# Ten RMS norms split between ScalarE and VectorE, eight layer norms reordered, and the last store cut in halves

## The reference, cut to what matters

```python
def layer_norm(x, g, b, eps=1e-5):
    mu = jnp.mean(xf, -1, keepdims=True)
    var = jnp.mean(jnp.square(xf - mu), -1, keepdims=True)
    return ((xf - mu) * lax.rsqrt(var + eps) * g + b).astype(x.dtype)

def rmsnorm(x, g):
    y = x32 * lax.rsqrt(jnp.mean(x32 * x32, axis=-1, keepdims=True) + RMS_EPS)
    return (y * g.astype(jnp.float32)).astype(x.dtype)
...
    x = layer_norm(ALPHA * x + mix, ln1_g[l], ln1_b[l])      # layers 0, 1
    x = layer_norm(ALPHA * x + ffn, ln2_g[l], ln2_b[l])
...
    h = rmsnorm(x, attn_norm[layer])                         # layers 2, 3
    x = x + mixed @ w_o[layer]
    h = rmsnorm(x, ffn_norm[layer])
    x = x + conv_ffn(h, w_up[layer], conv_w[layer], conv_b[layer], w_down[layer])
return rmsnorm(x, final_norm)
```

## Time and profile before

| | us |
|---|---|
| median of the runs | 1466.06 |
| the profiled execution, its own time | 1465.25 |
| its span in the trace | 1463.5 |
| TensorE busy | 1389.7 (95%) |
| VectorE busy | 976.4 (67%) |
| ScalarE busy | 700.4 (48%) |
| mean granted TensorE clock | 0.978 |

### The profile page before, as it was taken

The page is one execution under the profiler, slowest core; times in us unless marked ns, Lnnn a source line. Parts: engine busy times, 40 slices in busy tenths (PEclk is TensorE's granted clock), DMA queues, the critical chain, the costliest instruction groups (busy, mean ns, idle before and its releaser), DMA issues.

```text
span 1463.5 us, 24482 instructions
## 1 busy us (share of the span) xinstructions
PE 1389.7 (95%) x10006; PEld 1285.3 (88%) x10006; DVE 976.4 (67%) x1660; ACT 700.4 (48%) x1149; POOL 85.1 (6%) x79
## 2 busy tenths in 40 slices
PE   9998899999999898999998999999999999999997
PEld 7997689999899777999987998889998899889996
DVE  5766775555759466655565685787768555786777
ACT  4755444334385543434344544455545454454453
POOL 0320000000014000000000011120000000000000
PEclk9999999999999899999998999999999999999999
DMA  8742245555443213655533434345454433445441
GB/s 317 276 150 87 87 147 195 177 192 183 166 155 137 91 59 121 225 175 195 178 131 142 145 116 145 134 163 183 180 200 159 173 123 132 157 157 206 187 173 58
DMA packets 38343, 233.22 MB, mean 159 GB/s; under 512 B 4984, under 2 KB 8776, under 8 KB 11864
## 3 DMA queue, kind: packets, MB, share of 16 engines
q1 hardware_dynamic: 36168, 224.18, 43.2%
q0 software_dynamic: 2064, 7.47, 1.6%
HBM read 230.55 MB, written 1.09 MB: 158 GB/s over the span
## 4 chain that ended last, share of the span: by engine, by line
PE 82%; DVE 10%; ACT 4%; issue 2%; POOL 0%; DMA 0%; SPq 0%; DVEq 0%; ACTq 0%
PE bank L746 24%; PE bank L747 24%; PE bank L748 23%; DVE w_lo L582 2%; PE bank L850 2%; ACT w_hi L572 1%; PE bank L930 1%; PE bank L952 1%; PE bank L954 1%; PE bank L953 1%; DVE a_lo L603 1%; DVE nstat L1555 1%; PE bank L826 1%; DVE arena L1630 0%; ACT a_hi L598 0%
## 5 line engine op out<-in xcount | busy, mean ns | idle before, releaser
L582 DVE TENSOR_TENSOR w_lo<-raw,w_hi 128x1024 fp32r<-128x1024 f32 x404 | 484.9, 1237 | 97.4 <-ACT w_hi L572 94.2
L746 PE MATMUL bank<-a_hi,w_hi 128*128 128x256 f32 x1856 | 530.0, 286 | 3.1 <-DVE w_lo L582 3.1
L747 PE MATMUL bank<-a_lo,w_hi 128*128 128x256 f32 x1856 | 525.9, 283 | 0.0
L748 PE MATMUL bank<-a_hi,w_lo 128*128 128x256 f32 x1856 | 525.8, 283 | 0.0
L572 ACT ACTIVATE w_hi<-raw 128x1024 fp32r<-128x1024 f32 x404 | 406.3, 1050 | 97.6 <-PE bank L748 89.6
L746 PEld LDWEIGHTS bank<-a_hi,w_hi 128*128 128x128 f32 x1856 | 356.4, 192 | 7.4 <-issue 4.4
L747 PEld LDWEIGHTS bank<-a_lo,w_hi 128*128 128x128 f32 x1856 | 356.5, 192 | 1.3
L748 PEld LDWEIGHTS bank<-a_hi,w_lo 128*128 128x128 f32 x1856 | 356.6, 192 | 0.0
L746 PE MATMUL bank<-w_hi,a_hi 128*128 128x256 f32 (+1 forms) x512 | 168.8, 330 | 16.3 <-DVE a_lo L603 15.5
L747 PE MATMUL bank<-w_lo,a_hi 128*128 128x256 f32 (+1 forms) x512 | 161.8, 316 | 0.0
L748 PE MATMUL bank<-w_hi,a_lo 128*128 128x256 f32 (+1 forms) x512 | 161.3, 315 | 0.0
(11 more groups left out here) (248 smaller groups left out, 1484.4 us busy)
## 6 DMA issues: line engine op xcount, KB each, us to landing
raw<-in_stream SPq DMA_DIRECT2D x201, 1024.0 KB, 4.9
bias_t<-bias_rows SPq DMA_DIRECT2D x6, 512.0 KB, 7.0
heads_buf<-in_w SPq DMA_DIRECT2D x2, 1024.0 KB, 7.9
gains<-in_w SPq DMA_DIRECT2D x2, 1024.0 KB, 10.0
gains<-in_ln_g POOLq DMA_DIRECT2D x4, 512.0 KB, 3.9
gains<-in_ln_b POOLq DMA_DIRECT2D x4, 512.0 KB, 5.7
gains<-in_rms_g POOLq DMA_DIRECT2D x3, 512.0 KB, 3.8
res<-in_xT SPq DMA_DIRECT2D x4, 256.0 KB, 5.2
```

Source lines behind the costliest of these rows:

```text
L582: dve.tensor_tensor(w_lo[:, i % PARTS, half_tile(h)], raw[:, i % SLOTS, half_tile(h)], w_hi[:, i % PARTS, half_tile(h)].bitcast(F32), ALU. ...
L746: pe.matmul(out, lh, rh, start=first, stop=False)
L747: pe.matmul(out, lh, rl, start=False, stop=False)
L748: return pe.matmul(out, ll, rh, start=False, stop=last)
```

## The change

RMS norms (4 to 8): ScalarE squares each half and sums the squares along the row in the same instruction, takes the root, and scales the first half; VectorE makes the first half's share of the mean square plus epsilon (a 128x1 operation), multiplies the first half by the gain while ScalarE squares, inverts the root, and scales the second half. TensorE waits for the first half on a semaphore of its own. Layer norms (0 to 3): the pass that subtracts the mean and multiplies by the gain now stands ahead of the wait for the root. The last store is issued in four pieces of 256 KB, each as its half is done. POOL's wait ahead of a load of gains asks for the same event in the new count.

```diff
@@ scalar: root
+                if n < 4:
+                    act.wait_ge(sum_done, sum_done_at(n, tt))
+                    act.activation(st[:, 14:15], st[:, 13:14], ACT.Sqrt, bias=eps_ln[:, 0:1]).then_inc(root_done, 1)
+                    return
+                for hf in range(2):
+                    if n == 4:
+                        act.wait_ge(normed, normed_by(3, tt, hf))
+                    else:
+                        act.wait_ge(acc_drained, sum_of(n) * PIECES + piece(tt, hf))
+                    act.activation(res[:, tt, half_rows(hf)], x[:, tt, half_rows(hf)], ACT.Square,
+                                   accum_out=st[:, hf:hf + 1]).then_inc(squares_done, 1)
+                act.wait_ge(squares_done, 2 * rms_no(n, tt) + 2)
+                act.wait_ge(half_sum, rms_no(n, tt) + 1)
+                act.activation(st[:, 14:15], st[:, 1:2], ACT.Sqrt, scale=1.0 / D,
+                               bias=st[:, 2:3]).then_inc(root_done, 1)
+                act.wait_ge(half_scaled, rms_no(n, tt) + 1)
+                act.wait_ge(rstd_done, rms_no(n, tt) + 1)
+                act.activation(res[:, tt, half_rows(0)], res[:, tt, half_rows(0)], ACT.Copy,
+                               scale=st[:, 15:16]).then_inc(first_normed, 1)
@@ vector
+            def rms_norm(n, tt):
+                st, no = nstat[:, tt, :], rms_no(n, tt)
+                if n > 4:
+                    for hf in range(2):
+                        residual(n, tt, hf)
+                    dve.wait_ge(gains_in, 16 * (8 + n - 4))
+                else:
+                    dve.wait_ge(gain4_in, 16)
+                first, second = [gain4[:, half_rows(hf)] if n == 4 else gains[:, 0, half_rows(hf)] for hf in range(2)]
+                dve.wait_ge(squares_done, 2 * no + 1)
+                dve.tensor_scalar(st[:, 2:3], st[:, 0:1], 1.0 / D, 1e-6, ALU.mult, ALU.add).then_inc(half_sum, 1)
+                dve.tensor_tensor(res[:, tt, half_rows(0)], x[:, tt, half_rows(0)], first,
+                                  ALU.mult).then_inc(half_scaled, 1)
+                dve.wait_ge(root_done, root_at(n, tt))
+                dve.reciprocal(st[:, 15:16], st[:, 14:15]).then_inc(rstd_done, 1)
+                dve.wait_ge(rstd_done, no + 1)
+                dve.scalar_tensor_tensor(res[:, tt, half_rows(1)], x[:, tt, half_rows(1)], st[:, 15:16], second,
+                                         ALU.mult, ALU.mult).then_inc(normed, 1)
...
-                dve.wait_ge(root_done, sum_done_at(n, tt))
-                step(dve.reciprocal(st[:, 15:16], st[:, 14:15]))
...
+                    step(dve.scalar_tensor_tensor(res[:, tt, c], res[:, tt, c], st[:, 12:13], gains[:, 0, c],
+                                                  ALU.subtract, ALU.mult))
+                    if hf == 0:
+                        dve.wait_ge(root_done, root_at(n, tt))
+                        step(dve.reciprocal(st[:, 15:16], st[:, 14:15]))
+                    dve.scalar_tensor_tensor(x[:, tt, c], res[:, tt, c], st[:, 15:16], gains[:, 1, c], ALU.mult,
+                                             ALU.add).then_inc(normed, 1)
@@ sync
             for tt in range(NT):
-                sp.wait_ge(normed, 8 * PIECES + piece(tt, 1))
-                sp.dma_start(a["out"][:, tt, :], res[:, tt, :]).then_inc(out_sem, 16)
-            sp.wait_ge(out_sem, 16 * NT)
+                for hf in range(2):
+                    wait_normed(sp, 8, tt, hf)
+                    sp.dma_start(a["out"][:, tt, half_rows(hf)], res[:, tt, half_rows(hf)]).then_inc(out_sem, 16)
+            sp.wait_ge(out_sem, 16 * PIECES)
```

More of the change, by code:

```diff
@@ L483, in build @@
         normed = sem("normed")
+        first_normed = sem("first_normed")
+        squares_done = sem("squares_done")
+        half_sum = sem("half_sum")
+        half_scaled = sem("half_scaled")
+        rstd_done = sem("rstd_done")
         gains_in = sem("gains_in")
@@ L549, in normed_by, with rms_no, wait_normed, root_at @@
         def normed_by(n, tt, hf):
+            if n < 3:
+                return n * PIECES + piece(tt, hf)
             if n in (3, 4):
-                return 3 * PIECES + 4 * tt + 2 * (n - 3) + hf + 1
-            return n * PIECES + piece(tt, hf)
+                return 3 * PIECES + 3 * tt + (n - 3) + hf + 1
+            return 3 * PIECES + 3 * NT + NT * (n - 5) + tt + 1
+        def rms_no(n, tt):
+            return NT * (n - 4) + tt
+        def wait_normed(eng, n, tt, hf):
+            if n >= 4 and hf == 0:
+                eng.wait_ge(first_normed, rms_no(n, tt) + 1)
+            else:
+                eng.wait_ge(normed, normed_by(n, tt, hf))
         def sum_done_at(n, tt):
+            return n * NT + tt + 1
+        def root_at(n, tt):
             return 3 * NT + 2 * tt + n - 2 if n in (3, 4) else n * NT + tt + 1
@@ L1531, in choose, with residual @@
                     step(dve.match_replace(part, stat[:, 8:16], part, TAKEN))
+            def residual(n, tt, hf):
+                c = half_rows(hf)
+                at = sum_of(n) * PIECES + piece(tt, hf)
+                dve.wait_ge(acc_full, at)
+                acc = bank[:, 4 + 2 * tt + hf, :]
+                if n == 0:
+                    dve.wait_ge(x_rows_in, 2 * 16)
+                if 0 < n < 4:
+                    dve.wait_ge(normed, normed_by(n - 1, tt, hf))
+                if n < 4:
+                    dve.scalar_tensor_tensor(res[:, tt, c], x[:, tt, c], ALPHA, acc, ALU.mult,
+                                             ALU.add).then_inc(acc_drained, 1)
+                else:
+                    dve.tensor_tensor(x[:, tt, c], x[:, tt, c], acc, ALU.add).then_inc(acc_drained, 1)
+                return at
@@ L1533, in norm @@
             def norm(n, tt):
+                if n >= 4:
+                    rms_norm(n, tt)
+                    return
                 st = nstat[:, tt, :]
                 for hf in range(2):
[L1537 to L1554 removed]
@@ L1555, in norm @@
-                    ins = dve.bn_stats(st[:, 6 * hf:6 * hf + 6], rows)
-                step(ins)
-                if n < 4:
-                    dve.bn_aggr(st[:, 12:14], st[:, 0:12]).then_inc(sum_done, 1)
-                else:
-                    step(dve.bn_aggr(st[:, 12:14], st[:, 0:12]))
-                    dve.scalar_tensor_tensor(st[:, 13:14], st[:, 12:13], st[:, 12:13], st[:, 13:14], ALU.mult,
-                                             ALU.add).then_inc(sum_done, 1)
-                dve.wait_ge(root_done, sum_done_at(n, tt))
@@ L1565, in norm @@
-                step(dve.reciprocal(st[:, 15:16], st[:, 14:15]))
-                if n == 4:
-                    dve.wait_ge(gain4_in, 16)
-                else:
-                    dve.wait_ge(gains_in, 2 * 16 * (n + 1) if n < 4 else 16 * (8 + n - 4))
+                    dve.wait_ge(acc_drained, residual(n, tt, hf))
+                    ins = dve.bn_stats(st[:, 6 * hf:6 * hf + 6], res[:, tt, half_rows(hf)])
+                step(ins)
+                dve.bn_aggr(st[:, 12:14], st[:, 0:12]).then_inc(sum_done, 1)
@@ L1903, in next_gains @@
             def next_gains(n, g, b=None):
[L1904 removed]
+                pool.wait_ge(normed, normed_by(n - 1, NT - 1, 1))
                 load_gains(g, b)
```

35 lines of the change are left out of this document (3 added, 32 removed).

## The result

In the same comparison the kernel before took 1467.53 us (median of five runs, 1465.76 to 1473.11) and the changed one 1456.39 (five runs, 1455.92 to 1460.28). The ratio is 0.9922, with an interval of 0.9903 to 0.9942: 11 us less, where 6.6 were forecast. The changed kernel was measured twice more among the experiments, with ratios of 0.9933 and 0.9948, so its gain is better read as 0.5 to 0.8% than as this one number. The median of its 18 runs in the three comparisons is 1459.2 us.

A forecast was written before the change was run, and what follows sets the result against it. TensorE bounds the kernel (82% of the 1463.5 us span), so only its waits count. Savings of 3.4 + 0.3 + 0.7 + 1.2 + 1.0 = 6.6 us from 1465.25 give 1458.65, with the median's 0.81 1459.5; range 1456.5 to 1463.5.

The forecast's parts named there:

- norms 5 to 7: Token group 1's transposes behind these RMS norms start earlier, saving 3.4 us in three places, between 2.4 and 4.0.
- The saving of 1.14 a place: Norms 5, 6 and 7, group 1: transposes could start at 939.83 instead of 940.97, leaving 0.19 us of stall.
- a sign of being wrong that the prediction had named: The prediction is wrong if VectorE's multiplication by the gain holds up the inversion; running 0.1 longer delays it 0.1.
- Rival 3: ScalarE's 512-column instructions with sum or column scale run far slower than the copy: 1473 us; chance 0.04 with anything else slower.
- The clock: Behind norm 6, with the stall all but gone, the clock stays up: 1.0 us saved, between 0 and 1.4.
- Rival 1: The clock gives back more: one more fall avoided, such as norm 1 group 1, 2 us more, 1457.5; chance 0.2.
- The base: The profiled execution's 1465.25 us, with 0.81 added because the median stands that far above it.
- Norms 3 and 4: Group 0's transposes 1.5 us late behind ScalarE's splits, group 1's path shorter: 0.3 us saved, between -0.9 and 1.2.
- The end: Behind the last norm, earlier store issue (0.8) and a smaller last transfer (0.6): 1.2 us taken, between 0.8 and 1.4.
- the landing: Last store: landing takes 2.6 us again, and 256 KB less in the last transfer saves another 0.6 us.
- Layer norms: Root's wait hidden behind a pass, 0.32 us at each of three places; 0.7 us taken, between 0.5 and 1.0.
- Rival 4: VectorE multiplies faster, so halving the scaling gains nothing; norms 5 to 7 give 2.5, 1460.4 us; within the forecast's 0.55 chance.

The follow-up runs named there:

- filled: Extra identity products on TensorE ahead of norms' transposes: ratio 0.9933 (1461.7 us) added to the kernel before, 0.9911 (1457.05 us) added to the changed kernel.
- the kernel before again: The kernel before, executed once more with nothing changed: median 1470.11 us over 10 runs, ratio 1.0008, profiled span 1468.1 us.

## Why the prediction was right or wrong

**Where the difference lies.** The result of 1456.39 us is the profiled execution itself, 8.9 us less than the profiled execution before, where 6.6 were forecast: 2.3 of the 3.1 us between forecast and result. The other 0.8 is what the forecast added for the median. Of the 2.3, norm 1's clock gives +2.3, norm 6's +0.2, the other stretches +0.8, and the rest of the sum -1.0 together (end -0.5, norms 3 and 4 -0.3, layer norms -0.1, norms 5 to 7 -0.1).

**Direction and path: right.** Squares of 512 columns take 0.61 to 0.63 us with 0.19 for the read, 0.73 from start to start of what follows; the scaling by a column takes 0.72; the root 0.29. All were taken so. The saving of 1.14 a place came at norms 6 and 7 (1.15, 1.14); at norm 5 it was 0.99, since there the root stands at 936.06, 2.15 us behind the addition instead of 2.08, and the inversion at 936.48. VectorE's small operation starts only at 935.81 there, so the multiplication by the gain ends at 936.56, behind the root's end at 936.35, and the inversion comes 0.1 us late: a sign of being wrong that the prediction had named, though a small one. What holds the small operation up at norm 5 alone isn't shown. Three places: 3.3 us against 3.4. Rival 3, slow forms, is dead by the same rows.

**The clock: the step that failed.** It said of norm 6 that "with that stall all but gone I expect the clock to stay up, as it did behind norms 5 and 7 with the stall", and counted 1.0 us for it "between 0 and 1.4". The first half came true (1.2 us). What was wrong is "as it did behind norms 5 and 7": it took one execution's clock for the kernel's. In how many profiled executions the clock fell behind each norm, leaving out those that were filled there (norm 1 goes by the layer norms' order, norms 5 to 7 by the kind of RMS norm):

| place | us lost by a fall | old form | new form |
|---|---|---|---|
| norm 1 | 2.3 | 4 of 4 | 1 of 7, half as long |
| norm 5 | 1.25 | 1 of 4 | 0 of 9 |
| norm 6 | 1.2 | 3 of 4 | 0 of 9 |
| norm 7 | 1.3 to 1.5 | 3 of 4 | 0 of 9 |

The loss at norms 6 and 7 is the difference in the length of the same stretch between executions of the same form (norm 7: 34.7 us in the kernel before again, 33.4 in the first). On average the new RMS norms save 1.25 x 1/4 + (1.2 + 1.3) x 3/4 = 2.2 us of clock at norms 5 to 7, and the order of the layer norms 2.3 at norm 1, where the term had 1.0 for all. So the mis-sized term is the clock's: 1.0 us, against 3.5 at norms 1 and 6 in the first pair of profiles, and 4.5 on average by this table. With 3.3, 0.0, 0.6 (layer norms) and 0.7 (end) that makes 9.1 us, 0.62%, within all three measured intervals. The RMS part of it, 3.3 + 0.7 + 2.2 = 6.2, agrees with the 6.9 measured for it alone. The layer norms' part doesn't: 2.9 us should have shown, and the interval ends at 2.2. In that kernel's profiled execution norm 1 was 2.6 us shorter, and the stretch from 116 to 177 us, ahead of all norms, 6.3 us longer by low-clock stretches. Whether over its twelve runs that is chance isn't settled.

The table covers only what stands right behind the norms, and the traces of all kernels show two things beside it. First, from the table load ahead of norm 5 to 1442 us the nine executions with new RMS norms are 5.4 us shorter on average than the four unfilled ones with old norms, close to 3.3 + 2.2. That average has the falls elsewhere in it: three of the nine have one at 1283 to 1288 us, 1.4 us each, that none of the four has. Second, for the layer norms the wider view gives less. In three of the seven unfilled executions with the new order the stretch between norms 1 and 2 is 1.8 to 3.3 us longer (in the other four 0.9 shorter), so that from norm 0 to norm 2 the order saves 2.4 us on average and not 2.9. And all six falls at 117 us, ahead of norm 0, are in kernels with the new order (6 of 9, against 0 of 5 with the old); they make the stretch up to 177 us 2.4 us longer on average, which would undo the order's gain, as the ratio of 0.9999 for it alone has it. They lie ahead of every instruction that the change touches, and no run shows how the order could cause them; it may be chance.

Rival 1 is thus the case that occurred, and at the place it named; its 1457.5 is 1.1 from the first result. The result lies 0.1 us below the range's end, which took in most of that rival and not all. It had a chance of 0.2. A stall of 1.5 us is still longer than the 1.34 behind which norm 6's clock had fallen, and yet norm 1's clock held in six of seven: the length of the stall alone doesn't decide.

**The base.** "The median stands 0.81 above that execution" rested on three runs. All 69 runs of the kernel before in these comparisons have a median of 1469.6 us and lie between 1463.3 and 1476.3. The first three were at the low side, and the first five of the changed kernel (1456.39) below the 1459.2 of all its runs. So the forecast time of 1459.5 is close to that median, but by luck, since a base 3.6 us too low and a saving that was too small by nearly as much cancel.

**Norms 3 and 4: 0.3 expected, 0.0 between the two first profiles, 0.5 without the clock.** The reading was right: group 0's transposes later (forecast 1.5, the stall grew by 1.4), group 1's stall smaller by 1.6. Behind the table load the first matmul of group 0 is 19.3 - 18.6 = 0.7 later, and group 1's transposes are 30.92 - 30.38 = 0.5 earlier. Both figures repeat to 0.02 us in all profiled executions of the two kernels, three of each. The length of the whole stretch doesn't repeat: 52.0, 53.2 and 53.0 us in the kernel before (the last with the store cut), 52.0, 51.1 and 51.9 in the changed one, with 10.2 to 13.7 us at the lower clock. The 0.0 compares an execution with 10.2 such us to one with 13.7, which is the mistake of the clock term again, in reading the result. That the lateness came from the place in ScalarE's order is shown by moving the squares: 2.5 us back ahead of the first matmul.

**The end: 1.2 expected, 0.7 measured.** The steps to the scaling held (2.06 us from the second addition to the scaling, 2.0 forecast). The mis-sized term is the landing. I took 0.6 off for 256 KB less in the last transfer, but both halves are done at the same instant (1451.04 and 1451.07), so both pieces are under way at once, and the same 512 KB move behind two issues instead of one. A piece of 256 KB is listed with 2.5 us to its landing, one of 512 KB with 2.6: no run shows the 0.6. Measured, the cut costs 0.45 there.

**Layer norms: 0.7 expected, 0.6 in the stalls and lengths** (0.33, 0.22 and 0.05 us at norms 1, 0 and 2); the stall itself is 0.30 to 0.34 shorter at each, but where the clock is low for what follows little of it is left.

**Rival 4: half right.** The saving did not shrink to 2.5, since ScalarE scales in 0.72. But "nothing from halving" is what the run without it shows at norms 6 and 7: the transposes of the first half start as early either way. There all of the 1.14 comes from the statistics, whose 0.70 us passes stood between and behind the additions, while the first square runs beside the second addition on the other engine. At norm 4, of which the rival doesn't speak, halving is worth 0.65 us, and at norm 5 0.17. The Trainium skill's rule in "ScalarE: Activation LUTs", "Rules for kernel authors", to give multiplications to VectorE, with bf16 as its case, would have made the halved form the slower one. The trace doesn't bear that out here: for 128x512 float32 the rows show 0.72 against 0.75 us, and the halved form is nowhere slower by more than 0.03 us ahead of the transposes.

## What to carry to other kernels

Move a reduction to the engine that is idle beside the additions, so that it overlaps them; moving part of the final scaling as well bought nothing where the consumer only waits for the first half, and 0.65 us at the one norm where it soon waits for the engine that scales. Look at what the moved work now queues behind: one split tile more ahead of two squares cost 2.5 us at one norm. And read the clock from several executions before it goes into a sum: a stall just above a us costs its own length, and in some executions as much again in low clock behind it. Look at the whole trace when such a place is mended, not only at the place: falls came at others instead.

## What the runs showed of the hardware

- **The clock makes the spread.** Profiled executions of the kernel before differ by 4.6 us in span, while the stalls ahead of the norms' first transposes are the same to 0.04 us; all but 0.7 us of the difference (587 to 747 us, where the clock is high in both) lies in stretches with low clock in one or the other. Of the fourteen profiled executions of all kernels, seven came to the table load at 116 us at least 0.15 us later than the first one did, and in six of them the clock fell at about 117 us; in none of the seven others. It costs 1.6 to 6.3 us by 177 us. All this lies ahead of every instruction that the change touches (20 us from 117 on: 116 matmuls at a granted clock of 0.91 in the kernel before, 80 at 0.68 in the run without ScalarE's scaling).
- **Work that does nothing is worth time.** Ten products of 128 columns ahead of norm 0's transposes kept the clock at 2.4 GHz and gave 1.5 us in the kernel before, and did not delay the transposes. In the changed kernel the filled places gained as much, and another stretch lost 4.6 us.
- **Two stores issued together are slower than one of their size**: 6.31 us to the end against 5.86, here where both halves are ready at once.
